# Neighbourhood attention on one core: dense products at the end of a step and at other steps

## The reference, cut to what matters

```python
def hybrid_layer(x, norm_g, w_in, q_norm_g, k_norm_g, rpb, w_o_attn, w_o_na, w_out, cos, sin):
    h = rms_norm_2(x, norm_g)
    proj = jnp.einsum('bld,de->ble', h, w_in)
    qa, ka, va, za, qb, kb, vb, zb, ga, gb = split_cols(proj)
    ...
    oa = gqa_attention(qa, ka, va) * jax.nn.silu(za)
    ...
    ob = neighbourhood_attention(qb, kb, vb, rpb) * jax.nn.silu(zb)   # 8 heads of 64
    ya = jnp.einsum('ble,ed->bld', oa, w_o_attn)
    yb = jnp.einsum('ble,ed->bld', ob, w_o_na)
    mixed = jax.nn.sigmoid(ga) * ya + jax.nn.sigmoid(gb) * yb
    return x + jnp.einsum('bld,de->ble', mixed, w_out)

def neighbourhood_attention(q, k, v, rpb):
    ...  # a query sees 8 rows x 16 columns of the 8 x 64 grid, with a bias, and the 16 meta keys
    s = jnp.concatenate([s_win, s_meta], axis=-1)
    p = jax.nn.softmax(s, axis=-1)
    return einsum(p_win, v_win) + einsum(p_meta, vm)
```

## Time and profile before

| | us |
|---|---|
| Median of 3 runs (lowest, highest) | 1676.45 (1676.28, 1678.82) |
| The profiled execution: its own time | 1674.83 |
| The profiled execution: span of its instructions | 1673.5 |
| TensorE busy in the span | 1606.2 |
| VectorE busy in the span | 871.9 |
| ScalarE busy in the span | 633.4 |

### The profile page before, as it was taken

The page is one execution under the profiler, slowest core; times in us unless marked ns, Lnnn a source line. Parts: engine busy times, 40 slices in busy tenths (PEclk is TensorE's granted clock), DMA queues, the critical chain, the costliest instruction groups (busy, mean ns, idle before and its releaser), DMA issues.

```text
span 1673.5 us, 24837 instructions
## 1 busy us (share of the span) xinstructions
PE 1606.2 (96%) x10381; PEld 1356.3 (81%) x10381; DVE 871.9 (52%) x1558; ACT 633.4 (38%) x1124; POOL 50.4 (3%) x51
## 2 busy tenths in 40 slices
PE   7999978999999999999999999999999998999997
PEld 5898766677888888899888778999987887678886
DVE  4434666556644655855454455436555445545443
ACT  5232256443322334733344342223333343442333
POOL 0000001000000000020000000000020000000000
PEclk9999989899999999999999899999999999999999
DMA  6234400024233322332112102223422113113231
GB/s 196 76 80 89 113 14 14 14 88 119 84 100 101 101 80 96 99 67 76 51 51 49 54 14 77 77 89 120 96 51 76 51 37 51 54 39 101 89 113 51
DMA packets 175600, 125.22 MB, mean 75 GB/s; under 512 B 48752, under 2 KB 172272, under 8 KB 175488
## 3 DMA queue, kind: packets, MB, share of 16 engines
q1 hardware_dynamic: 175488, 123.63, 26.5%
HBM read 121.52 MB, written 2.10 MB: 74 GB/s over the span
## 4 chain that ended last, share of the span: by engine, by line
PE 89%; DVE 4%; ACT 4%; issue 2%; DMA 1%; SPq 0%; POOL 0%; DVEq 0%; ACTq 0%; POOLq 0%
PE bank L586 69%; PE bank L2743 2%; PE bank L2775 2%; PE bank L2755 2%; PE bank L3151 1%; ACT w_hi L533 1%; PE bank L2651 1%; PE bank L2602 1%; PE bank L1602 1%; DVE w_lo L542 1%; PE bank L1658 1%; PE bank L3114 1%; PE bank L1478 1%; ACT probs L1532 1%; PE bank L3130 1%
## 5 line engine op out<-in xcount | busy, mean ns | idle before, releaser
L586 PE MATMUL bank<-h_hi,w_hi 128*128 128x512 f32 (+2 forms) x920 | 327.4, 376 | 7.6 <-issue 4.4
L542 DVE TENSOR_TENSOR w_lo<-w_raw,w_hi 128x2048 fp32r<-128x2048 f32 (+2 forms) x117 | 241.2, 2061 | 177.0 <-ACT w_hi L533 176.4
L586 PE MATMUL bank<-h_lo,w_hi 128*128 128x512 f32 (+2 forms) x920 | 322.6, 370 | 0.0
L586 PE MATMUL bank<-h_hi,w_lo 128*128 128x512 f32 (+2 forms) x920 | 321.2, 369 | 0.0
L533 ACT ACTIVATE w_hi<-w_raw 128x2048 fp32r<-128x2048 f32 (+2 forms) x117 | 201.1, 1719 | 74.4 <-DMA w_raw<-w_in 36.0
L586 PEld LDWEIGHTS bank<-h_hi,w_hi 128*128 128x128 f32 (+1 forms) x920 | 166.9, 189 | 49.9 <-issue 16.6
L586 PEld LDWEIGHTS bank<-h_hi,w_lo 128*128 128x128 f32 (+1 forms) x920 | 166.6, 189 | 30.6 <-issue 0.2
L586 PEld LDWEIGHTS bank<-h_lo,w_hi 128*128 128x128 f32 (+1 forms) x920 | 166.5, 189 | 30.1 <-issue 0.5
L586 PE MATMUL bank<-g_hi,w_hi 128*128 128x264 f32 (+1 forms) x752 | 183.0, 309 | 1.4 <-DVE z_a L2225 0.9
L586 PE MATMUL bank<-g_lo,w_hi 128*128 128x264 f32 (+1 forms) x752 | 180.8, 306 | 0.0
L586 PE MATMUL bank<-g_hi,w_lo 128*128 128x264 f32 (+1 forms) x752 | 180.4, 306 | 0.0
(11 more groups left out here) (574 smaller groups left out, 2633.1 us busy)
## 6 DMA issues: line engine op xcount, KB each, us to landing
w_raw<-w_in SPq DMA_DIRECT2D x45, 1024.0 KB, 5.3
w_raw<-w_up SPq DMA_DIRECT2D x32, 512.0 KB, 4.9
w_raw<-w_in SPq DMA_DIRECT2D x40, 256.0 KB, 4.5
w_raw<-w_down SPq DMA_DIRECT2D x8, 1024.0 KB, 5.1
w_raw<-w_out SPq DMA_DIRECT2D x8, 1024.0 KB, 5.1
w_raw<-w_out SPq DMA_DIRECT2D x8, 512.0 KB, 3.4
w_raw<-w_ple_gate SPq DMA_DIRECT2D x4, 1024.0 KB, 5.1
w_raw<-w_o_attn SPq DMA_DIRECT2D x8, 512.0 KB, 3.5
```

Source lines behind the costliest of these rows:

```text
L542: DV.e.tensor_tensor(wlo[u % RING][:, 0:n], raw[u % RING][:, 0:n], whi[u % RING][:, 0:n].bitcast(F32), ALU.subtract).then_inc(*w_low(u))
L586: ins = PE.e.matmul(out, stationary[a](k), moving[b](k)[i], start=first and n == 0, stop=last and n == 2)
```

## The change

The dense products in the neighbourhood stage move to the end of a step (after the value) on all three engines, and to other steps. `places_in_na` gives the item behind whose score, turn and value the product comes; since the loop tests `step - 1 in places`, the products stand at the end of steps 1, 6, 10, 14 in layer a and 1, 4, 6, 10, 12, 14 in layer b. Both splits of the second z half move into its last step. `pe_nsa` of the first block is written out with its order unchanged, and `filled` gets a list of places whose default gives the same steps as before.

```diff
+        def filled_last(items, fill, places, score, turn, value):
+            for step in range(len(items) + 3):
+                for stage_, behind in ((score, 0), (turn, 2), (value, 3)):
+                    if 0 <= step - behind < len(items):
+                        stage_(items[step - behind])
+                if step - 1 in places:
+                    next(fill)
             drain(fill)
...
-        split_in_z = [(1, 3), (2, 3)]
+        split_in_z = [(1, 3), (3, 3)]
...
-                if k in split_in_z[half_]:
+                for _ in range(split_in_z[half_].count(k)):
                     ac_split()
...
-                if k in split_in_z[half_]:
+                for _ in range(split_in_z[half_].count(k)):
                     dv_split()
...
-            filled(items_a, all_of(fill, first_steps(mix, mixed_in_na(l))), 2 + mixed_in_na(l), score, turn, value, apart=True)
+            filled_last(items_a, all_of(fill, first_steps(mix, mixed_in_na(l))), places_in_na(l), score, turn, value)
...
+        def places_in_na(l):
+            return (0, 3, 5, 9, 11, 13) if layers[l].last else (0, 5, 9, 13)
```

More of the change, by code:

```diff
@@ L715, in first_steps, with filled @@
                 yield next(steps)
-        def filled(items, fill, total, *stages_, apart=False):
+        def filled(items, fill, total, *stages_, places=None):
             given = [0]
+            places = places or [-(-(n + 1) * len(items) // total) - 1 for n in range(total)]
+            assert len(places) == total
             def give(item):
-                n = items.index(item) + 1
-                while given[0] < total * n // len(items):
+                while given[0] < total and places[given[0]] <= items.index(item):
                     next(fill, None)
@@ L728, in first @@
                 give(item)
[L730 to L733, removed]
+            pipeline(items, first, *stages_[1:])
+            drain(fill)
+        def filled_last(items, fill, places, score, turn, value):
[5 more added lines that the diff above has]
+                    next(fill)
             drain(fill)
@@ L1726, in pe_nsa @@
             fill = pe_mlstm_out_steps()
-            filled(units_n, first_steps(fill, 11), 11, pe_nsa_score, pe_nsa_turn, pe_nsa_value, apart=True)
+            given = 0
+            for step in range(len(units_n) + 3):
+                if step < len(units_n):
+                    pe_nsa_score(units_n[step])
+                while given < 11 * min(step, len(units_n)) // len(units_n):
+                    next(fill)
+                    given += 1
+                if 0 <= step - 2 < len(units_n):
+                    pe_nsa_turn(units_n[step - 2])
+                if step > 2:
+                    pe_nsa_value(units_n[step - 3])
             for t, br, j0 in units_n[-2:]:
```

## The result

| | us | ratio to before (95%) |
|---|---|---|
| Before, median beside the changed kernel | 1678.04 | |
| Changed kernel, median of 5 runs (lowest 1690.99) | 1692.59 | 1.0097 (1.0077 to 1.0118) |
| Changed kernel again, first repeat | 1686.44 | 1.0104 (1.0069 to 1.0138) |
| Changed kernel again, second repeat | 1691.32 | 1.0092 (1.0065 to 1.0118) |

The change makes the kernel 1.0% slower, 16.3 us by the ratio and 14.6 between the two medians; 11 were forecast. The ratio leaves out one execution of the kernel before (3445.82 us) and one of the changed kernel (2631.97 us, at a granted clock of 0.553 throughout), and since the profile of the changed kernel is of that one, the profile after is taken from the two repeats, here called first repeat (span 1684.4, clock 0.985) and second repeat (span 1691.2, clock 0.979).

A forecast was written before the change was run, and what follows sets the result against it. TensorE was taken as the bound, 89% of the chain that ended last. 1674.83 + 4.9 (waits) + 6 (clock) = 1685.7, raised 1.6 to the runs' median: 1687.4 us, 0.65% slower, chance 0.45; range 1677.5 to 1696.

The forecast's parts named there:

- What is removed: TensorE's idle time in both stages plus layer a's half-clock opening: 8.7 us in layer a, 3.6 in layer b.
- The turns: Turns of items 6, 10 and 14 wait bare for VectorE's multiplication: 1.49, 1.81 and 2.84 us idle in each layer.
- Third pair of scores: At each layer's opening, item 3 waits for meta scores and meta maximum: about 0.6 us.
- step 4 of layer b: VectorE does two splits ahead of reading the product's bank: 2.2 us idle, 1.1 with one split.
- step 12: In layer b, item 13 stands behind the reading of the product's bank: 0.95 us idle.
- The pair of splits in layer a: Same two splits as in layer b, said to end 0.25 us late, inside slack: no cost.
- The sum of the waits: Layer a 7.0 us against 8.7 removed, layer b 10.2 against 3.6: together 4.9 us slower at an undisturbed clock.
- The clock behind item 14: Clock falls behind item 14's wait in both layers: two falls at 3 us each, 6 us.
- one: Rival: the clock holds and only the waits count, 1681.4 us; chance 0.22.
- Two: Rival: each tile's multiplication is ready when its turn comes, in both layers; 7.3 us faster, 1669.1 us; chance 0.08.
- Three: Rival: the clock falls at nearly every wait, six times at 3 us, 1699.4 us; chance 0.10.
- four: Rival: clock holds, each of the seven large waits is 0.4 us shorter; no measurable change, 1678.6 us; chance 0.15.

The follow-up runs named there:

- warm_14: Changed kernel with three extra 512-column matmuls ahead of item 14's turn in each layer, filling its wait; 1681.41 us, 1.0049 to the kernel before.
- warm_open: Kernel before with one extra matmul in each layer, inside the 1.48 us wait behind the first pair of scores; 1673.54 us, 0.998.
- one_split: Changed kernel with the splits of the second z half back in steps 3 and 4, one each; 1688.01 us, 1.006 to the kernel before.
- between: Changed kernel's steps, but each dense product except the first stands between score and turn, not at the step's end; 1695.85 us, 1.0115 to the kernel before.
- warm_all: Changed kernel with extra matmuls ahead of the turns of items 6, 10 and 14 and layer b's fourth pair of scores; 1684.41 us, 1.0048 to before.
- last_at_16: Changed kernel with each layer's last dense product back in step 16 between score and turn; 1676.11 us, 1.0017 to the kernel before.
- both_covers: Kernel before with first product ending step 1, layer b's others ending steps 6 and 10, rest between score and turn at 8, 12, 16; 1670.03 us, 0.9979.
- first_only: Kernel before with only the first dense product of each layer moved, to the end of step 1; 1672.31 us, 0.9973.
- both_covers_2: Second run of the same kernel as both_covers, for a closer ratio; 1670.99 us, 0.9963 to the kernel before.

## Why the prediction was right in its waits and too low in its sum

1. That a microsecond in the stages is one at the end: right. The dense runs behind keep 176.08 and 144.61 us; a fall that reached into one added 1.1. The span less the two stages and the clock's losses outside them is 1490.2 us before, 1490.5 and 1490.9 in the repeats and 1490.7 in warm_14, and 1487.6 to 1490.6 in the other traces (worked out from the table).
2. What is removed: right. No idle time at the opening, clock 1.00, no wait for a tile's copy, none of 0.74. The half clock of the opening is taken away in the traces (4.57 us lost in the profiled execution, 4.4 forecast). What comes back is less, because the wait ahead of the third pair of scores, which the half clock had hidden, comes out (0.49 us in warm_open), as the forecast has it in its 0.6: warm_open gives 3.77 us in layer a of its trace and 3.4 over the executions.
3. The turns: right. 1.36 and 1.68 us in each layer (1.49 and 1.81 forecast) and 2.81, 2.79 (2.84), released by the multiplication at L2735. Third pair of scores 0.50 (0.6), step 4 of layer b 2.18 (2.2), step 12 0.79 (0.95). The pair of splits in layer a was not inside slack: it made 0.49 us ahead of items 8 and 9, where 0.16 stood, and in one_split, without the pair, 0.16 stands again.
4. The sum of the waits: layer a without any fall 87.65 us (warm_14) against 89.81 less 4.57, so +2.4 where −1.7 + 4.4 = +2.7 was said; layer b 85.79 against 79.48, +6.3 where 6.6 was said. Together 8.7 against 9.3.
5. The clock behind item 14: **the term that was too small.** A fall behind these waits was right, its size was not. The text took 3 us each, and two falls, 6 us. The four traces with a bare wait there (both repeats, one_split, between) have eight such waits. Seven fell, for 3.08, 3.08, 6.25, 6.12, 4.71, 6.33 and 4.78 us, one did not: 4.3 a wait, 8.6 a kernel, and 8.0 by the ratios of the changed kernel and warm_14. The row taken for it had 6.7 us of half clock with 6.53 busy; here it lasted some 7 us in two places and 10 to 14 in five. The text counted on some 6 us of small matmuls to be slowed; in the longest falls the dense product behind them ran at half clock as well.
6. What is left. Of the 16.3 us, 8.0 is item 14's clock (6 forecast) and 8.2 the rest (4.9 forecast), by warm_14's ratio, whose interval is 5.4 to 11.1. The stages in the traces account for 4.1 of the rest (8.7 − 4.57), so some 4 us more are missing. They have no place in the waits of the stages, and they are missing in other kernels too: warm_all's stages are 4.1 us longer than before and it measures 8.0 more, last_at_16's are 1.6 shorter and it measures 2.8 more, both_covers' are 8.1 shorter and it gains 3.5. Less is missing in first_only (6.3 shorter, gains 4.5) and in the second run of both_covers (8.1 shorter, gains 6.2), and nearly nothing in warm_open (3.8 shorter, gains 3.4). The kernel before has a single trace, in which the clock fell in layer a's opening and took less outside the stages (14.0 us) than in any other. Its executions spread: beside both_covers_2, 6 of 17 took 1671.3 to 1673.7 us and 11 took 1676.2 to 1682.7. If in some of them the clock does not fall in the opening, up to 3.8 us of the remainder would be that. It isn't shown, and it can't be all of it, since warm_open and warm_all were compared with the same executions. The remainder stays open.

So the forecast was too low by 5.4 us (16.3 against 10.9): 2.0 in item 14's clock (8.0 against 6) and 3.3 in the rest, where the stages came out 0.8 us under their 4.9 and the remainder of 4 us had no term. The measured median of 1692.59 lies just above the 1683.5 to 1692 of the forecast itself and inside 1677.5 to 1696. How near it came is in part luck, since the falls differ from one execution to the next: the first repeat lost 3.08 us at item 14 in both layers together, the second 9.3.

The rivals: one (the clock holds, 1681.4) is out as a cause of the total, since warm_14 and last_at_16 each give back what it denies. Two is out: no multiplication was ready. Three fell with warm_all and with the count of falls behind the shorter waits, four with the lengths of the waits, none of which came 0.4 us shorter.

The Trainium skill, "TensorE: Matmul & The Clock Gate", section "A second HAM failure mode: psum-queue depth-cycling", has frequent short idle times swing the clock. The runs agree in part: seven of eight waits of 2.8 us, but two of 28 waits of 1.3 to 2.2 us, were followed by a fall, and filling the shorter ones bought nothing that can be measured (1.0049 and 1.0048).

## What to carry to other kernels

A filler in a software pipeline pays by what it lies over: name for every product the wait that it covers, and the step in which that wait falls, before moving it; here a product in the wrong step bared waits of 1.4 to 2.8 us. Count what VectorE reads for the filler as well, since it is queued ahead of the very result that TensorE waits for. A wait among small matmuls may cost more in clock than in idle time (here 8.0 us against twice 2.8), and a spare matmul in it is a cheap way to measure that, and at times to keep it.

## What the runs showed of the hardware

- A fall of the clock behind a wait of 2.8 us is neither sure nor of one length: at one place with the same instructions it was absent once (layer a, first repeat) and 3.08 us once (second repeat); in layer b 3.08 and 6.25. In all, seven of eight such waits were followed by a fall, of some 7 to 14 us.
- TensorE stayed at 1.2 GHz while it was busy: from 1509 to 1523 us (second repeat) it was busy 12.82 of 14.00 us at a clock of 0.51, and from 1454 to 1458 without a break at a mean clock of 0.57.
- Half of the clock's losses of this kernel or more (14 to 21 us) lie outside the two stages. They differ by 7 us among the twelve traces and by 3.9 between the two of one kernel (16.9 and 20.8, both_covers); a difference of 3 us between two single profiles proves nothing before the stage's own length is read.
